# A trunk layer with mixer and experts: value biases, router products, expert biases and residual scale moved between engines

## What is computed

```python
h = layer_norm(x, ln_in_g, ln_in_b)
proj = h @ w_in + b_in             # lru_x, lru_gate, sq, sk, sv, bq, bk, bv
y = concat(group_rms(rg_lru(...)), group_rms(sliding_window(sq, sk, sv)), group_rms(stick_breaking(bq, bk, bv)))
h = layer_norm(2**0.25 * h + (y @ w_out + b_out), ln1_g, ln1_b)
logits = h @ w_router + b_router   # top 4 of 32, softmax over them
hb = h[tokens] @ w_exp_in[e] + b_exp_in[e]
ff = sum over the 4 experts of gate * (swiglu(hb) @ w_exp_out[e] + b_exp_out[e])
out = layer_norm(2**0.25 * h + ff, ln2_g, ln2_b)
```

## Time and profile before

| | |
|---|---|
| time before, median of 3 runs | 1474.34 us (1472.99 to 1474.62) |
| the profiled execution | 1474.43 us, its span 1472.7 us |
| mean granted TensorE clock | 0.991 |
| PE busy | 1427.1 us (97%) |
| DVE busy | 1214.7 us (82%) |
| ACT busy | 975.7 us (66%) |
| POOL busy | 490.6 us (33%) |

### The profile page before, as it was taken

How to read it: one execution, slowest core, us unless ns; L and a number is a source line. 1 busy time by engine, 2 the same in 40 slices (tenths; PEclk the granted TensorE clock), 3 DMA queues, 4 the chain that set the end, 5 groups by cost and what they waited for, 6 DMA issues and landing times.

```text
span 1472.7 us, 20375 instructions
## 1 busy us (share of the span) xinstructions
PE 1427.1 (97%) x6495; PEld 1095.9 (74%) x6495; DVE 1214.7 (82%) x1002; ACT 975.7 (66%) x710; POOL 490.6 (33%) x309
## 2 busy tenths in 40 slices
PE   6999989998999999999999999999999999999995
PEld 3466554776888888888888888888888888888873
DVE  5533357577999999999999999999999999999985
ACT  2244660176777777777777777777777777777762
POOL 4200125152333334344333444443343333333101
PEclk9999999999999999999999999999999999999997
DMA  7221226479999999999999999999999999999933
GB/s 260 76 61 36 61 104 261 186 270 360 367 378 379 377 386 385 380 377 371 376 378 384 379 380 390 385 387 382 381 380 378 379 378 381 379 379 378 359 122 126
DMA packets 86310, 461.43 MB, mean 313 GB/s; under 512 B 11912, under 2 KB 26506, under 8 KB 37130
## 3 DMA queue, kind: packets, MB, share of 16 engines
q1 hardware_dynamic: 75190, 431.91, 74.6%
q0 software_dynamic: 9648, 26.49, 7.8%
q10 hardware_dynamic: 1444, 2.66, 0.7%
HBM read 443.92 MB, written 25.76 MB: 319 GB/s over the span
## 4 chain that ended last, share of the span: by engine, by line
PE 75%; DVE 1%; DMA 1%; POOL 1%; issue 1%; POOLq 0%; DVEq 0%; ACT 0%; ACTq 0%
PE banks L1765 69%; PE banks L1733 2%; PE banks L1739 2%; DMA acc_dram<-glu_lin 1%; PE banks L1797 1%; POOL sel L1464 1%; PE banks L1860 0%; POOLq L1466 0%; DVE raw L1694 0%; PE banks L1865 0%; DVEq L1585 0%; DVE raw L1698 0%; PE banks L1727 0%; DVE glu_lin L1581 0%; ACT hi L1352 0%
## 5 line engine op out<-in xcount | busy, mean ns | idle before, releaser
L1544 DVE TENSOR_TENSOR lo<-raw,hi 128x2048 fp32r<-128x2048 f32 x384 | 867.1, 2289 | 75.8 <-ACT hi L1352 75.5
L1352 ACT ACTIVATE hi<-raw 128x2048 fp32r<-128x2048 f32 x384 | 733.7, 1920 | 249.6 <-PE banks L1765 249.4
L1765 PE MATMUL banks<-hi,x_hi 128*128 128x512 f32 x1040 | 286.7, 397 | 8.8 <-DVE x_lo L1568 6.5
L1765 PE MATMUL banks<-lo,x_hi 128*128 128x512 f32 x1040 | 280.1, 391 | 0.0
L1765 PE MATMUL banks<-hi,x_lo 128*128 128x512 f32 x1040 | 278.9, 389 | 0.0
L1464 POOL TENSOR_SCALAR sel<-cst,rank_e 128x128 bf16<-128x128 f32 x120 | 209.7, 1759 | 136.9 <-issue 136.9
L1765 PEld LDWEIGHTS banks<-lo,x_hi 128*128 128x128 f32 x1040 | 195.9, 188 | 41.9
L1765 PEld LDWEIGHTS banks<-hi,x_lo 128*128 128x128 f32 x1040 | 195.4, 188 | 41.4
L1765 PEld LDWEIGHTS banks<-hi,x_hi 128*128 128x128 f32 x1040 | 190.7, 188 | 47.3 <-issue 11.2
L1487 POOL DMA_INDIRECT acc_dram<-ye,dst_row x31 | 50.2, 1620 | 363.5 <-ACT ye L1377 363.5
L1765 PE MATMUL banks<-hi,a_hi 128*128 128x512 f32 x496 | 155.7, 395 | 0.0
(11 more groups left out here) (276 smaller groups left out, 1198.5 us busy)
## 6 DMA issues: line engine op xcount, KB each, us to landing
raw<-in_w_exp_in SPq DMA_DIRECT2D x256, 1024.0 KB, 7.7
raw<-in_w_exp_out SPq DMA_DIRECT2D x128, 1024.0 KB, 7.2
raw<-in_w_in SPq DMA_DIRECT2D x9, 1024.0 KB, 7.6
raw<-in_w_out SPq DMA_DIRECT2D x4, 1024.0 KB, 5.1
x<-in_x SPq DMA_DIRECT2D x4, 512.0 KB, 6.2
h_dram<-x SPq DMA_DIRECT2D x4, 512.0 KB, 3.2
bias_in<-bias_dram SPq DMA_DIRECT2D x128, 3.0 KB
raw<-acc_dram SPq DMA_DIRECT2D x4, 512.0 KB, 5.3
```

The costliest lines, as they stand in the source:

```text
L1352: act.activation(hi[:, c0 % PARTS, :], raw[:, c0 % RAW, :], ACT.Copy).then_inc(hi_done, 1)
L1544: dve.tensor_tensor(lo[:, c0 % PARTS, :], raw[:, c0 % RAW, :], hi[:, c0 % PARTS, :].bitcast(F32), ALU.subtract).then_inc(lo_done, 1)
L1765: last = pe.matmul(psum[:, bank + n, :], s[:, k, :], w[:, at:at + 512], start=(first and m == 0 and new), stop=(closes and m == steps - 1 ...
```

## The change

- The one-row products of `bv0`, `bv1` and `sv` go. `vrow` is loaded to all 128 partitions, and VectorE adds the bias while it moves the bank to `vpad` or `vdup` (two operations a job), at the job's place in `STEPS`. ScalarE waits for it (`v_added`) and only then signals `job_copied` and goes on.
- The router's products are turned: `w_rt` is stationary, `h1T` moves (128 columns), the result has the experts on the partitions. ScalarE adds the bias as it copies it (`logitT`), TensorE turns it back (`turn_logits`). Another `keep_busy(4)` stands before the last turn.
- The source of the bias split lies in `y`; SyncE starts its transfers, half 0 before chunk 5, half 1 before chunk 7 after a wait for the split of half 0; GpSimd splits after the masks of heads 0 and 1; ScalarE waits for the second split before `g0`, which writes to `y`.
- GpSimd makes gain * 2**0.25 and shift * 2**0.25 + b_out before its passes; VectorE's four passes at L836 go.

```diff
+                    if g == 5:
+                        load_biases(0)
+                    if g == 7:
+                        sp.wait_ge(bsrc_free, 1)
+                        load_biases(1)
...
@@ ScalarE, job()
-                    elif kind == "bv":
-                        ...
-                            last = act.activation(dst[:, :, :, b, 64 * b:64 * b + 64], src[:, :, :, b, :], ACT.Copy)
+                    elif name in ("bv0", "bv1", "sv"):
+
+                        act.wait_ge(v_added, ("bv0", "bv1", "sv").index(name) + 1)
+                        act.sem_inc(job_copied, 1)
+                        return
...
+                        if n == "g0":
+                            act.wait_ge(bsrc_free, 2)
...
-                        load_biases(0)
...
-                act.wait_ge(bsrc_free, 1)
-                load_biases(1)
...
+                    for j in ((i - 2,) if i < NT else (i - 2, i - 1)):
+                        if j >= 0:
+                            act.wait_ge(rt_in, 32)
+                            act.wait_ge(rtT_ready, j + 1)
+                            act.activation(logitT[:, P * j:P * j + P], psum[0:E, 7, P * j:P * j + P], ACT.Identity,
+                                           bias=b_rt[:, :]).then_inc(rtT_copied, 1)
@@ GpSimd
+                pool.tensor_scalar(gain_b, gain_b, ALPHA_DN, None, ALU.mult)
+                pool.tensor_scalar(shift_b, shift_b, ALPHA_DN, None, ALU.mult)
+                pool.drain()
+                pool.tensor_tensor(shift_b, shift_b, bout_b[:, :], ALU.add)
...
-                    if h >= 2:
-                        split_biases(h - 2)
+                    if h < 2:
+                        split_biases(h)
@@ VectorE
+                    elif what == "job" and n[:2] == "bv":
+                        dve.wait_ge(job_ready, JOB[n] + 1)
+                        dve.wait_ge(zeroed, 1)
+                        dve.wait_ge(row_in, 16 * 3)
...
+                        for b in range(2):
+                            last = dve.tensor_tensor(dst[:, :, :, b, 64 * b:64 * b + 64], src[:, :, :, b, :],
+                                                     bias[:, :, b, :].unsqueeze(1).broadcast_to([P, 2, 2, 64]), ALU.add)
+                        last.then_inc(v_added, 1)
                     elif (what, n) == ("job", "sv"):
-                        dve.wait_ge(job_copied, JOB["sv"] + 1)
+                        dve.wait_ge(job_ready, JOB["sv"] + 1)
...
+                        for b in range(2):
+                            last = dve.tensor_tensor(vdup[:, :, :, 64 * b:64 * b + 64], src, bias, ALU.add)
+                        last.then_inc(v_added, 1)
+                        dve.drain()
...
-                for i in range(NT):
-                    dve.scalar_tensor_tensor(x[:, i, :], x[:, i, :], ALPHA_DN, bout_b[:, :], ALU.mult, ALU.add)
-                dve.drain()
@@ TensorE
-                            last = pe.matmul(o, ones[0:1, :], vrow[0:1, row:row + width], start=False, stop=True)
...
-                    o = psum[:, 6, E * i:E * i + E]
+                    o = psum[0:E, 7, P * i:P * i + P]
                     for k in range(KD):
-                        pe.matmul(o, h1T[:, k, P * i:P * i + P], w_rt[:, k, :], start=(k == 0), stop=False)
-                    last = pe.matmul(o, ones[0:1, :], b_rt[:, :], start=False, stop=True)
+                        last = pe.matmul(o, w_rt[:, k, :], h1T[:, k, P * i:P * i + P], start=(k == 0), stop=(k == KD - 1))
+                    last.then_inc(rtT_ready, 1)
+
+                def turn_logits(i):
+
+                    pe.wait_ge(rtT_copied, i + 1)
+                    last = pe.transpose(psum[:, 6, E * i:E * i + E], logitT[:, P * i:P * i + P], ident[0:E, 0:E])
...
                 project_all(3)
+                turn_logits(0)
                 route(1)
                 turn_h1(2)
                 pe.wait_ge(out_added, 2 * NT)
                 keep_busy(4)
+                turn_logits(1)
                 route(2)
                 turn_h1(3)
                 keep_busy(4)
+                turn_logits(2)
                 route(3)
+                keep_busy(4)
+                turn_logits(3)
                 keep_busy(13)
```

More of the change, by code:

```diff
@@ L403, in _, with load_biases @@
                     sp.dma_start(x[:, i, :], t["x"][P * i:P * i + P, :]).then_inc(x_in[i], 16)
+                def load_biases(h):
+                    for m in range(3):
+                        sp.dma_start(bsrc[E * m:E * m + E, :], t["b_exp_in"][:, F * h:F * h + F]).then_inc(bsrc_in, 16)
                 for g in range(MIX_CHUNKS):
+                    if g == 5:
[3 more added lines that the diff above has]
+                        load_biases(1)
                     if g == 1:
                         sp.dma_start(relb[:, :], t["rel_bias"]).then_inc(rel_in, 16)
[L407 to L408 removed]
+                        for at, first_col, n in ((0, 1408, 128), (128, 2048, 256)):
+                            src = bass.AP(tensor=t["b_in"].tensor, offset=t["b_in"].offset + first_col, ap=[[0, P], [1, n]])
+                            sp.dma_start(vrow[:, at:at + n], src).then_inc(row_in, 16)
                         sp.dma_start(wrg[:, :, :, :], t["w_rg"]).then_inc(row_in, 16)
@@ L500, in job @@
                                                   bias=vec[r, V_BIN + 10:V_BIN + 11])
[L501 to L504, removed]
                     elif kind == "x":
@@ L532, in job @@
                     last.then_inc(job_copied, 1)
-                def load_biases(h):
-                    for m in range(3):
-                        act.dma_start(bsrc[E * m:E * m + E, :], t["b_exp_in"][:, F * h:F * h + F]).then_inc(bsrc_in, 16)
                 for what, n in STEPS:
@@ L1011, in job @@
                     if name[:2] in ("bv", "sv"):
-                        tiles, lo, width, row = (range(2 * half, 2 * half + 2), 0, 256, 128) if name[0] == "b" else (
-                            range(NT), 128, 128, 0)
+                        tiles, lo, width = (range(2 * half, 2 * half + 2), 0, 256) if name[0] == "b" else (range(NT), 128, 128)
                         for m, i in enumerate(tiles):
@@ L1017, in job @@
                             for k in range(KD):
-                                pe.matmul(o, hT[:, k, P * i:P * i + P], w[:, k, lo:lo + width], start=(k == 0), stop=False)
-                            last = pe.matmul(o, ones[0:1, :], vrow[0:1, row:row + width], start=False, stop=True)
+                                last = pe.matmul(o, hT[:, k, P * i:P * i + P], w[:, k, lo:lo + width], start=(k == 0),
+                                                 stop=(k == KD - 1))
                     else:
```

22 lines of the change are left out of this document (13 added, 9 removed).

## The result

The changed kernel takes 1478.80 us (median of 8 runs, 1477.57 to 1479.69) against 1474.48 for the kernel before in the same comparison (8 runs, 1472.99 to 1476.05): ratio 1.0027, 95% interval 1.0016 to 1.0037, or 4.3 us slower. The forecast was 1477.2, with "the same" (up to 0.2%) as the likeliest class; by that bound it came out just on the slower side. Its profiled execution took 1477.63 us, span 1475.8.

The account below looks back on a forecast made before the run. The prediction took TensorE as the bound, with GpSimd's mask releases at heads 0 and 1 as the tight places. Its terms, 1.3 + 0.2 + 0.1 + 0 + 1.4 + 0.7 - 0.3 - 0.6 = +2.8, gave 1477.2 us, range 1474.0 to 1481.0.

Parts of the forecast that it names:

- Head 0's release: At head 0's value product: ScalarE's wait for VectorE's adds delays the mask, +1.3 us with some 3.8 us of TensorE idle.
- Clock after the first idle: Behind head 0's idle: TensorE's granted clock most likely falls to half for a stretch, +1.4 us (0 to 1.7).
- What the removed products freed: TensorE before heads 0 and 1: removed one-row products free 2.5 us at bv0 and bv1, about 1.6 at sv.
- rival 3: At the value products: the mask's release is not late, so TensorE gains its 2.5 and 1.6 us; 1469.4 us, chance 0.09.
- Head 1's collision: At head 1's mask: VectorE's two shift copies start some 0.2 us after GpSimd's mask passes; +0.2 us (0 to 1.2).
- Clock after the second idle: Behind the 2.4 us idle ahead of head 1: the clock may go either way, half a fall, +0.7 us (0 to 1.7).
- g0's wait for the second split: ScalarE's g0 waits for the second bias split, ending about 158.6; +0.1 us, up to 0.6 if the copies delay it.
- Front: GpSimd's three added passes ahead of the convolutions: VectorE held about 1 us of each one-input pass, r0 unmoved; 0 us.
- rival 1: At the front: one-input GpSimd passes hold VectorE all 2.77 us, TensorE waits at r0 and r2; +3.7, 1480.9 us, chance 0.13.
- Router: At the router's end: -0.3 us for route(0)'s one-row product and -0.6 if turned products keep the clock.
- Rival 2: At both mixer idle times: waits only, the clock does not fall; +0.7, 1475.1 us, chance 0.13.
- Rival 4: In the router: turned products don't hold the clock, +1.4 us on the forecast, 1478.6 us, chance 0.05.

Follow-up runs that it names:

- e4: Changed kernel with ScalarE issuing its four band DMAs before its wait for VectorE's adds of bv0; 1475.84 us, ratio 0.9999 to the kernel before.
- e6: Changed kernel with 15 and 13 products on constants filling TensorE's idle times ahead of the value products of heads 0 and 1; 1478.25 us, ratio 1.0024.
- e8: e4 plus the LRU's sqrt and scans for head 1 (step lru 1) moved ahead of the sk product's copies; 1468.72 us, ratio 0.9962.
- e7: Changed kernel with VectorE's two shift copies of vdup held until GpSimd's mask of head 1 is done; 1479.79 us, ratio 1.0028.
- e1: Kernel before with the value part alone: bv0, bv1 and sv without one-row products, VectorE adding the biases; 1478.33 us, ratio 1.0024.
- e9: Kernel before with only the two moves of e8 (band DMAs and step lru 1 earlier), nothing of the change; 1473.66 us, ratio 0.9994.
- e10: e8 with the router part of the change undone; 1467.33 us, ratio 0.9956.
- e2: Changed kernel with the value part undone (one-row products and ScalarE's copies back); 1475.18 us, ratio 0.9999.
- e5: Kernel before with the router part of the change alone; 1476.54 us, ratio 1.0009.
- e11: e8 with 4, 9 and 25 products on constants ahead of head 0, the squares and the second expert's products; 1465.44 us, ratio 0.9937.
- e3: Changed kernel with 29 and 26 products on constants in the idle times ahead of heads 0 and 1, too many to fit; 1478.84 us, ratio 1.0026.
- e12: e8 without the keep_busy(4) ahead of the last turn_logits; 1467.46 us, ratio 0.9953.

## Why the prediction was right, and where it was not

The time lies in the range and 1.6 us above the point. The main mechanism was right: the one-row products bought no time, since the masks' release was late and got later. Step by step, in us behind bv:

- **Head 0's release**: forecast +1.3 with an idle of 3.8; measured 29.32 - 28.30 = +1.0 with 4.14. The adds take 0.75 for two. e4 shows the queue behind ScalarE's wait as the cause.
- **Clock after the first idle**: forecast +1.4. From the value product to sq1 it was 4.32 us (113.10 to 117.42) before and 6.11 after (113.75 to 119.86): +1.8, just above its upper bound of 1.7. e6 shows the idle as the cause.
- **What the removed products freed**: forecast 2.5 us at bv and 1.6 at sv. TensorE took 17.00 us from the first bv product to the suffix sums behind them before and 13.82 after, and 9.55 and 7.31 for sv: 3.2 and 2.2 us. Since the release set the time, this did not enter the sum, but it lengthened both idle times, and rival 3 should have had 5.4 us to gain and not 4.1. In e8 4.1 of the 5.4 reach head 1; 1.24 are still idle at head 0.
- **Head 1's collision**: forecast +0.2 between 0 and 1.2, near the free end because the mask starts first. The copies started first, by 0.09 us, and the mask lost 0.78. This term was mis-sized; e7 confirms cause and size. The subtraction moved with everything else, so how two operations 0.1 us apart fall could not be told, and the middle of the bounds was the better choice.
- **Clock after the second idle**: forecast +0.7, half of a fall. From the value product to g0 4.42 before, 6.06 after: +1.6. The idle was 3.74 us, where I had 2.4: 0.71 as before, 2.24 freed by sv and 0.78 from the collision. So it stood near the first idle, and the half of a fall was mis-sized.
- **g0's wait for the second split**: forecast +0.1; nothing, the delay is the same ahead of g0 and behind it (4.87 and 4.88 us on the clock of the trace). Later on came 0.4 more ahead of head 2 (its idle 1.77 us) and 0.2 at the squares (an idle of 2.57 for the 2.29 of the earlier trace rows), of which I had nothing.
- **Front and rival 1**: 0 as forecast. A 4-column step of VectorE was held 0.94 us beside a 2.79 us pass.
- **Router**: forecast -0.9, measured +0.2 in the changed kernel (+6.1 in all, +5.9 ahead of the projection at 222.48). This step failed. The fall that went was worth 0.9, more than the -0.6 I had for it, but I put that fall down to the 32-column products, and that did not bear out: e1, e9 and e10 have those products and no fall. The failing term is the other one: where the clock holds either way the part costs 1.2, where I had -0.3 and a top-8 0.8 late, +0.5 together. The rows show where: TensorE waits 0.46 us for ScalarE's copy twice, then 1.16 us of keep-busy products and a turn stand between the last logits and the top-8, although ScalarE was done 0.56 us earlier (290.73 + 0.36 against 291.65).

These sum to +6.1 against my +2.8: collision +0.6, clock +1.3, router +1.1, head 2 and the squares +0.6, less 0.4 at head 0 and g0. That the point missed by 1.6 only is luck: the expert stage gave part back, which I had ruled out by moving it as one block. In the profiled pair bv started 0.4 earlier and the span grew by 3.1, so 2.6 went behind the selection. The place is TensorE's first product on the reloaded sums: before, show 2.21 us of idle ahead of 1445.16; after there is none.

```profile
1448.86 1.88 PE L1894 MATMUL banks<-raw,cst 128*128 128x512 f32 x4
```

Before, that product started 6.51 us after SyncE's reload was issued (1438.65); in the changed kernel it started 4.18 us after it (1444.68). The four kernels without the value part (before, e2, e5, e9) wait there 2.2 to 3.5 us in their profiled executions; of the ten with it only e6 does, 2.66. Reload to landing takes 3.2 to 7.1 us before and 3.3 to 6.9 after, so the transfers as such are no faster. Why the first product finds its data earlier was not tested and stays open, as does how often each kernel's clock falls in executions that have no profile.

Rival 2 (waits only, 1475.1) fell by the clock in both places, rival 3 (faster) by the idle times; e8 gives what rival 3 wanted, by other means. Rival 4 names 1478.6 us, nearest to the 1478.80 measured, but only by chance: its condition, a fall in the router, was not there (the 26 products took 3.17 us).

## What to carry to other kernels

Work taken from an engine that soon waits for another one turns into idle time. First count the slack to the next release (0.8 us at head 0 here, none at head 1, where TensorE already waited 0.71 us) and shorten the chain to it; otherwise the removal is worth no more than that slack. When the copy of a bank is handed to another engine, all that stands behind the wait in the first engine's queue moves too; four DMA issues of 2.46 us moved ahead of the wait gave back all of the delay at head 0 and more. A new idle of some 4 us on TensorE should be charged twice, as waiting and as half clock behind it. A few products on constants in it keep the clock, counted at two instructions each; what that is worth in the run's time is a second question, 0.4 to 0.6 us in e6 and 3.3 in e11.

## What the runs showed of the hardware

- **Falls of the clock are not a function of the idle alone.** An idle of 2.57 us ahead of the squares left the granted clock at 1.00 in after, e3 and e6 and was followed by 0.50 in e4, e7, e8 and e12; one of 2.29 us left it at 1.00 in before, e1, e2 and e9 and was followed by 0.50 in e5. Those of 4.14 and 3.74 us were followed by 0.50 each time they occurred (after, e1, e7; 3.74 also in e4), and so was the one of 2.95 us ahead of head 1 in e7. A fall costs 1.6 to 1.8 us under streaming products, 2.6 in the longer one of e4 (value product to g0 7.06 us against 4.42), and 0.9 at the end of the router.
- **VectorE's copies and GpSimd block each other, whichever comes first.** The four mask instructions take 1.03 us alone and 1.81 beside two copies that started 0.09 us earlier (after); a copy that takes 0.56 us took 2.38 when it started 0.41 us into a two-input GpSimd pass of 2.37 (e7). This fits the Trainium skill (SBUF — State Buffer, Who interferes with whom), where copies can take the port pair shared with GpSimd and whoever issues first has it for the whole instruction. It does not fit the small tensor_scalar in the front, held 0.94 us of a one-input pass of 2.79 that had started 0.13 us earlier; there the measurement decides, and the prediction went by it.
